# Experts stage: the last unit's gate and up weights in two row buffers, and the residual put on PSUM during the routing

## The reference, cut to what matters

```python
alpha = DEEPNORM_ALPHA            # 4 ** 0.25
for i in range(DEPTH):            # DEPTH = 2
    h = layer_norm(alpha * h + mix, ln_g[i, 0], ln_b[i, 0])
    h = layer_norm(alpha * h + memory_cross_attention(...), ln_g[i, 1], ln_b[i, 1])
    h = layer_norm(alpha * h + hierarchical_moe(h, ...), ln_g[i, 2], ln_b[i, 2])

def hierarchical_moe(...):        # top-2 of the experts of the best group
    ...
    for e in range(N_EXPERTS):
        hid = jax.nn.silu(t @ w_gate[e]) * (t @ w_up[e])
        y = y + combine[:, e:e + 1] * (hid @ w_down[e])
```

## Time and profile before

| | |
|---|---|
| median of 3 runs | 1701.95 us |
| the runs | 1703.22, 1698.22, 1701.95 us |
| span of the profiled execution | 1698.5 us |
| PE busy | 1658.8 us, 98% of the span |
| experts of layer 0 (first gate matmul to last scatter) | 1036.6 to 1263.3 us of the span |
| experts of layer 1 | 1460.4 to 1687.7 us |
| mean DMA traffic over the span | 219 GB/s |
| DMA traffic in the experts | about 425 GB/s |

### The profile page before, as it was taken

One profiled execution on the slowest core, in us unless ns is written; L12 is line 12 of the kernel. 1 busy time (PEld: TensorE's weight loads), 2 busy tenths in 40 slices (PEclk: granted clock), 3 DMA queues, 4 the chain that ended last, 5 costly groups with the idle time before them and its releaser, 6 DMA issues.

```text
span 1698.5 us, 30157 instructions
## 1 busy us (share of the span) xinstructions
PE 1658.8 (98%) x12820; PEld 1291.2 (76%) x12820; DVE 907.2 (53%) x1942; ACT 698.0 (41%) x1347; POOL 5.0 (0%) x6
## 2 busy tenths in 40 slices
PE   9999999999999999999999999999989999999996
PEld 8889999787698699999887986555546798655553
DVE  6676656644466456568658774232136876523213
ACT  5576444422343345455557553111123655311111
POOL 0000000000000000000000000000000000000000
PEclk9999999999999999999999999999999999999998
DMA  8613453433200554434451555999992355599995
GB/s 340 248 75 150 164 208 139 156 110 138 89 3 28 211 185 177 195 130 178 188 198 45 197 198 202 428 425 422 427 414 84 105 197 196 217 425 426 422 426 236
DMA packets 36443, 373.80 MB, mean 220 GB/s; under 512 B 7232, under 2 KB 8384, under 8 KB 11728
## 3 DMA queue, kind: packets, MB, share of 16 engines
q1 hardware_dynamic: 33216, 366.18, 54.1%
q10 hardware_dynamic: 3088, 5.61, 1.0%
HBM read 370.73 MB, written 1.05 MB: 219 GB/s over the span
## 4 chain that ended last, share of the span: by engine, by line
PE 89%; DVE 5%; DMA 3%; ACT 1%; issue 1%; DVEq 0%; SPq 0%; ACTq 0%
PE ps L655 41%; PE ps L2357 12%; PE ps L2380 6%; PE ps L879 3%; DMA ring<-in_w_moe 3%; PE ps L2343 2%; PE ps L1000 2%; PE ps L2369 2%; PE ps L1536 2%; PE ps L1780 2%; PE ps L1749 2%; PE ps L981 1%; PE ps L432 1%; PE ps L2845 1%; PE ps L1763 1%; PE ps L2411 1%
## 5 line engine op out<-in xcount | busy, mean ns | idle before, releaser
L655 PE MATMUL ps<-ffn_x_h,ffn_w 128*128 128x256 f32 x1408 | 257.4, 283 | 0.2
L2357 PE MATMUL ps<-ring,expert_inputs 128*64 128x256 f32 x2048 | 235.1, 382 | 0.5 <-DMA ring<-in_w_moe 0.3
L655 PEld LDWEIGHTS ps<-ffn_x_h,ffn_w 128*128 128x128 f32 x1408 | 221.3, 192 | 1.5 <-DVE ffn_x_l L494 0.5
L647 ACT CAST w_h<-ring 128x512 fp32r<-128x512 f32 x240 | 149.3, 624 | 138.1 <-PE ps L655 130.1
L650 DVE TENSOR_TENSOR w_l<-ring,w_h 128x512 fp32r<-128x512 f32 x240 | 164.2, 690 | 66.0 <-ACT w_h L647 62.0
L655 PE MATMUL ps<-ffn_x_l,ffn_w 128*128 128x256 f32 x704 | 199.2, 283 | 0.0
L2357 PEld LDWEIGHTS ps<-ring,expert_inputs 128*64 128x64 f32 x2048 | 141.3, 137 | 69.8 <-DMA ring<-in_w_moe 0.7
L650 DVE TENSOR_TENSOR ffn_w<-ring,ffn_w 128x1024 fp32r<-128x1024 f32 x132 | 155.8, 1221 | 20.8 <-ACT ffn_w L647 20.8
L655 PE MATMUL ps<-w_h,x_h 128*128 128x512 f32 x384 | 150.1, 391 | 0.0
L655 PE MATMUL ps<-w_h,x_l 128*128 128x512 f32 x384 | 149.5, 389 | 0.0
L655 PE MATMUL ps<-w_l,x_h 128*128 128x512 f32 x384 | 149.4, 389 | 0.0
(11 more groups left out here) (374 smaller groups left out, 2662.0 us busy)
## 6 DMA issues: line engine op xcount, KB each, us to landing
ring<-in_w_moe SPq DMA_DIRECT2D x64, 2048.0 KB, 14.6
ring<-in_w_proj SPq DMA_DIRECT2D x37, 2048.0 KB, 7.9
ring<-in_w_ffn SPq DMA_DIRECT2D x22, 3072.0 KB, 10.0
ring<-in_w_moe SPq DMA_DIRECT2D x64, 1024.0 KB, 15.4
ring<-in_w_b_in SPq DMA_DIRECT2D x1, 2496.0 KB, 18.3
ring<-in_w_lora SPq DMA_DIRECT2D x1, 2048.0 KB, 8.1
rows<-in_ln_g SPq DMA_DIRECT2D x4, 512.0 KB, 3.5
rows<-in_ln_b SPq DMA_DIRECT2D x4, 512.0 KB, 5.2
```

What stands on the lines that cost most here:

```text
L647: act.copy(high, x).then_inc(ready.up(), 1)
L655: last = pe.matmul(out, a[x], b[y], start=start and n == 0, stop=stop and n == 2, skip_group_check=True)
L2357: last = pe.matmul(bank(0)[g * SLOTS_E:(g + 1) * SLOTS_E, 0:2 * P], x[:, k, e * SLOTS_E:(e + 1) * SLOTS_E], wg[:, g, k, :], start=(k == 0) ...
```

## The change

- The gate and up weights of unit 31 don't go through the ring. During the routing SP loads the gate half into `rows` (1 MB) once the projection before has ended, and the up half into `h` (1 MB) once `h` has been transposed and split; it then enters its loop, which loads gate and up only to unit 30. The waits for the ring's slots are counted anew (`turns`). Unit 31 waits for a signal of its own (`late_in`).
- The residual no longer comes from `h`. 16 matmuls put `alpha * x` on banks 4 to 7: stationary is a 128x128 block of `xT`, moving is `alpha` times the identity, 128 columns. Four stand between the parts of the logits (L2260) and their gathering (L2265), four right behind L2265, eight behind a new wait of PE on DVE's read of the logits (`logits_read`, L2543). 5 fillers stand behind them in place of 11. `alpha` is made at the start of the stage on ACT, not behind the second exponential.
- The four `add_rows` matmuls (L2283) of units 27 to 30 are gone, so is DVE's `scale` at n = 9, and so are the loads of its rows in the cross attention's projection (L824, of both layers). The scatters add onto the banks from the first on; the first gather goes to banks 0 to 3.
- `load_rows` (ACT) moves from n = 16 to n = 31.
- In `dense` (not run here) the transposes of the scaled rows go away and the last four units are written out.

```diff
@@ project in cross_attention
-            project(2, residual=ALPHA, row_src=(d["ln_g"][3 * layer + 1], d["ln_b"][3 * layer + 1]), norm=from_rows(o))
+            project(2, residual=ALPHA, norm=from_rows(o))
@@ weights
+                last_gate, last_up = [x.rearrange("p (k n) -> p k n", k=KD) for x in (rows.rearrange("p a f -> p (a f)"), h.rearrange("p t f -> p (t f)"))]
                 def gate_up_weights(j):
-                    return ring[:, j % SLOTS, 0:DOWN_AT].rearrange("p (g k n) -> p g k n", g=2, k=KD)
+                    if j == j0 + EU - 1:
+                        return last_gate, last_up
+                    w = ring[:, j % SLOTS, 0:DOWN_AT].rearrange("p (g k n) -> p g k n", g=2, k=KD)
+                    return w[:, 0], w[:, 1]
@@ routing on PE, behind the parts of the logits
+                    def residual(t, ks):
+                        for k in ks:
+                            pe.matmul(bank(4 + 2 * t + k // 4)[:, (k % 4) * P:(k % 4 + 1) * P], xT[:, k, t * P:(t + 1) * P], alpha, start=(k % 4 == 0), stop=False, skip_group_check=True)
+                    pe.wait_ge(alpha_ready.sem, alpha_ready.at(1))
+                    residual(1, range(4))
                     pe.wait_ge(logits_in.sem, logits_in.at(1))
                     for t in range(T):
                         last = pe.matmul(bank(4)[:, t * ROUTE:(t + 1) * ROUTE], parted[:, t * P:(t + 1) * P], gather4, start=True, stop=True)
                     last.then_inc(mm.up(), 1)
-                    fill(pe, 11)
+                    residual(1, range(4, KD))
+                    pe.wait_ge(logits_read.sem, logits_read.at(1))
+                    residual(0, range(KD))
+                    fill(pe, 5, 2)
@@ the loop over the units
-                            arrived(pe, j0 + n)
+                            if n < EU - 1:
+                                arrived(pe, j0 + n)
+                            else:
+                                pe.wait_ge(late_in.sem, late_in.at(32))
...
-                            if RESIDUAL_AT <= n < RESIDUAL_AT + len(QUARTERS):
-                                add_rows(*QUARTERS[n - RESIDUAL_AT])
@@ ACT
-                            if n == 16:
+                            if n == EU - 1:
                                 load_rows(act)
@@ DVE
-                            if n == 9:
-                                scale(dve)
@@ SP
+                    last_unit = loads[j0 + EU - 1]
+                    sp.wait_ge(*end["dve"])
+                    sp.dma_start(rows.rearrange("p a f -> p (a f)"), last_unit[:, 0:2 * D]).then_inc(late_in.up(16), 16)
+                    tp = sig("transposed")
+                    sp.wait_ge(tp.sem, tp.at(KD))
+                    sp.wait_ge(low.sem, low.at(T))
+                    sp.dma_start(h.rearrange("p t f -> p (t f)"), last_unit[:, 2 * D:4 * D]).then_inc(late_in.up(16), 16)
                     for n in range(SLOTS, EU + 1):
-                        if n < EU:
+                        if n < EU - 1:
                             sp.wait_ge(gu.sem, gu.at(n - SLOTS + 1))
                             load_gate_up(sp, j0 + n)
```

More of the change, by code:

```diff
@@ L214, in build_program, with turns @@
         release = {}
+        last_units = {a + EU - 1 for a in moe_at}
+        def turns(j):
+            return j // SLOTS + 1 - sum(x <= j and x % SLOTS == j % SLOTS for x in last_units)
         def load(sp, j):
@@ L2435, in _ @@
                 def _(act):
+                    act.activation(alpha, ident[:], ACT.Copy, scale=ALPHA).then_inc(alpha_ready.up(), 1)
                     norm_act(act, own_norm)
```

77 lines of the change are left out of this document (31 added, 46 removed).

## The result

The changed kernel takes 1688.04 us (median of 5 runs, 1686.38 to 1689.56), the kernel before 1700.52 us on the same chip (5 runs, 1698.22 to 1703.22): ratio 0.9935, 95% interval 0.9924 to 0.9946. The forecast was 1693.8 us with a range of 1689.6 to 1699.2. The direction was right.

A forecast was written before the change was run, and what follows sets the result against it. PE was taken to set the experts' pace, the weight stream just touching it at unit 27. Gains of 3.9 us (layer 0) and 4.3 us (layer 1), together 8.2, gave 1701.95 - 8.2 = 1693.8 us, range 1689.6 to 1699.2.

The forecast's parts named there:

- The difference carries over: Whole kernel: the runs' median stays 3.45 us above the traced span, so 1701.95 - 8.2 = 1693.8 us.
- The transfers in the loop: Expert units 27 to 31: weights land before PE wants them, so removing four residual matmuls gains 4.24 us per layer.
- the last margin: Layer 1, unit 30: gate and up land about 0.2 us before PE wants them.
- The wait at unit 27: Experts, unit 27: PE's present wait for weights goes, gaining 0.07 us in layer 0 and 0.34 us in layer 1.
- Early loads, `load_rows`, `scale`, projection: Routing, unit 31 and cross attention's projection: the moved or removed loads and DVE's scaling change the time by 0.
- Rival D: End of layer 1: gain and bias rows arrive late, 1697.3 us at 14.4 us landing, up to 1705.1 us; chance 0.04.
- C: Routing: small transfers wait for the `rows` half, 1696.3 to 1698.7 us, shown by landing after 7.4 us; chance 0.08.
- The routing: Four residual matmuls before the gathering delay it and all behind it, 0.39 us in layer 0, 0.3 us in layer 1.
- B's first half: Layer 0's routing, 1030 to 1035 us: the clock dip goes, at most 1.7 us, 1692.1 us; chance 0.17 both ways.
- the closed gap before the gathering of the logits: Routing, before L2265: residual matmuls fill PE's 0.50 us gap, which by the skill's page speaks for the clock dip going.

The follow-up runs named there:

- megabyte_16: The changed kernel with 1 MB of extra row loads by ACT at n = 16: 1694.79 us, ratio to the kernel before 0.9973.
- weights_at_31: The changed kernel with unit 31's gate and up loaded into the two row buffers in the ring's turn, not in the routing: 1691.52 us, ratio 0.9963.
- residual_alone: The changed kernel with unit 31's weights through the ring again, no early loads and `load_rows` back at n = 16: 1698.08 us, ratio 0.9999.
- residual_dummy_loads: residual_alone plus the two early loads of 1 MB each in the routing, whose data nobody reads: 1699.4 us, ratio 0.9996.
- root_fill_outside: The changed kernel with ACT's table load ahead of the copies of `h` and 5 fillers behind the branch's end: 1691.5 us, ratio 0.9960.
- fill_between: The changed kernel with 10 fillers behind the last scatter of each layer, inside the branch: 1690.23 us, ratio 0.9945.

## Why the prediction was right or wrong

**The step that failed.** The forecast took one execution of before as the kernel's fixed time, and changed only what the change touches. "The difference carries over" put the runs 3.45 us above the span, where they stand 1.7 to 2.0 us above it; and everything outside the change was put at nothing without a reason. The way from the forecast span of 1690.3 us to the traced 1685.7 is, from the table: 3.5 us in code that the change does not touch (2.6 ahead of the first routing product, 0.9 between the layers), 2.0 us in the two routings (0.7 of it charged for the later gathering, the rest mostly the fall of the clock that was taken as it is), and 0.8 us the other way, unit 27 to 31 of layer 1. The stretches up to unit 27 make up the last 0.1 us. The anchor adds 1.6 us, and the median of the five runs lies 0.5 us above the profiled one: 4.6 + 1.6 - 0.5 are the 5.8 us between forecast and result, to rounding. The sum's own mechanism holds: 8.2 us forecast, 8.5 at equal clock. That the time fell so far below the range is in part the luck of the first five runs; the mean of all 16 is 1689.5 us, at its edge.

**The transfers in the loop: right.** "The loop is PE's alone, 4.24 us are gained": 27 to 31 went from 30.0 to 25.8 us in five of the six layers in the traces of after. The sixth (layer 1 of the first trace) waited 0.69 us, where the forecast had the last margin at 0.2 us. megabyte_16 shows that the megabyte moved out of n = 16 opened this room, weights_at_31 that the 2 MB of unit 31 did too (3.1 us of waiting when they stay in the stream), and residual_alone that without less traffic the residual's move is worth 0.1 to 0.5 us per layer in the loop.

**The wait at unit 27: right.** 0.07 and 0.34 us were charged (the timeline of layer 0 has 0.13); the three traces of after have no wait there, and unit 0 to 27 in layer 1 went from a mean of 184.9 to 184.6 us.

**Early loads, `load_rows`, `scale`, projection: right at nothing.** In layer 1, where it counts, the loads of the gain and bias rows at n = 31 landed in 3.4 and 4.6 us (5.2 assumed); in layer 0, where the reader comes much later, they took 9.7 and 16.4 us. DVE's L569 follows its predecessor with no wait. Rival D did not occur. (That 14.4 us stand against 22.2 for the ring's, which the prediction takes as a sign of queues that take turns, compares 0.5 MB with 2 MB and says little.) For the early loads the cost of nothing is right and the reason half wrong: the `rows` half did slow the small transfers that go ahead of it, by 1.2 and 2.0 us (residual_alone against residual_dummy_loads), and POOL's subtraction hid it. The sign that the prediction names for C, over 7.4 us to landing, was no sign: before shows 7.42 to 7.98 us in layer 1 in its four traces.

**The routing: its term was wrong in size.** The step "the gathering comes 0.39 us later, and all that hangs on it" failed at its second half. What hung on it was already waiting for POOL. The term is 0, within 0.1 us, and not 0.7. The views to see it in were there: a DVE instruction of 0.75 us whose twins take 0.17, in the same timeline as the earlier trace rows.

**The clock: the rival's sign was right, its weight and its reach were wrong.** B's first half (the fall of the gathering goes) happened; it is worth 0.9 us net and not 1.7: 1.4 us up to unit 0, of which DVE takes 0.5 back behind it. The text treated this stretch as the only place where the clock could differ. The traces show three (the mixer of layer 0, the gathering, between the layers), in each of which traces of one kernel differ by 1 to 2 us. The prediction weighed a page of the Trainium skill here (TensorE: Matmul & The Clock Gate, Part 1), by which the closed gap before the gathering of the logits speaks for the fall to go. residual_alone closes the same gap, and the clock fell in both its traces: that gap did not decide it.

**The anchor: wrong by 2 to 3 us.** "The median of the runs stands 3.45 us above the span; the difference carries over." In all 80 runs of the two kernels whose span is known the time is 1.7 to 2.0 us above the span. The rest of the 3.45 was that the profiled execution and the median of three were different draws. The mean of 64 runs of before is 1699.3 us and not 1701.95. From 1699.3 the sum gives 1691.1; after's 16 runs have a mean of 1689.5.

**The range.** It allowed 2.5 us for a median of a few runs, but took before's three as the reference. Spans of before reach from 1694.1 to 1701.8 us; both kernels' draws enter a comparison with few runs. Added up: 8.2 forecast, +0.7 for the routing; at the same clock 8.5 were measured; about 3 us are the clock of the first five runs of after against before's usual one, and about 1 us is where the five runs of before fell.

## What to carry to other kernels

Where two resources run within half a microsecond of each other, make the sum for both: here the PE half and the DMA half are worth nothing alone and 8.5 us together, since each half runs into the resource that the other relieves. Before charging a delay to everything behind it, look in the timeline for instructions longer than their twins: they may be waiting too, and their slack absorbs the delay. Anchor a small forecast on the span and clock of many executions, not on the median of three: spans of the kernel before lay up to 7.7 us apart, going with the granted clock.

## What the runs showed of the hardware

- The mean granted clock of one kernel on one core lay between 0.989 and 0.995 from run to run (64 and 16 runs), 1.4 us for each 0.001. It fell to 0.5 at a few places of the program, and in some of them in some executions only, with PE equally busy ahead of it (7.11 and 7.13 us of 8).
- A two-input DVE instruction started beside POOL's subtraction ended with it, at 0.75 and 0.45 us where 0.17 is usual; it shows as a longer instruction, with no idle time ahead.
- The last of three small transfers took 7.3 and 7.9 us to land when 1 MB was issued behind it on the same queue (residual_dummy_loads), 6.1 and 5.9 us without (residual_alone).
- PE's first instruction behind the branch of the experts started 5.2 us after its last inside, with nothing to wait for that the profile shows (root_fill_outside); with 4.6 us of fillers at the end of the branch, 2.35 us after the last filler (fill_between).
- In the experts the weights streamed at 425 GB/s on one core. The Trainium skill (DMA: Bandwidth & Descriptors, Specifications) gives some 358 GB/s as a NeuronCore's HBM limit, and further down, under Bandwidth, 425 GB/s for one core that streams alone. This kernel runs on one core, and its trace agrees with the second.
